# Cached values streamed 256 columns at a time against zero-padded probabilities

## The reference

```
z = rms_norm(x) @ w_in           # q, k, v: 12 heads of 64; GLU value and gate; two branch gates
A = merged attention of 3 groups of 4 heads, (window, dilation) = (128,1), (512,4), (2048,16); @ w_att
B = GLU -> causal depthwise conv (31) -> layer norm -> silu -> @ w_conv_out
x = x + (sigmoid(ga) * A + sigmoid(gb) * B) @ w_out
x = x + SwiGLU(rms_norm(x))
# for the samples, per group g, with cached and new keys and values behind each other:
idx = L + arange(S)[:, None] - dil * arange(window // dil + 1)[None, :]
s = einsum('bshd,bsjhd->bshj', q, k[:, idx]) * HEAD_DIM ** -0.5
o = einsum('bshj,bsjhd->bshd', exp(s - lse), v[:, idx])
o_att = sum over groups of softmax(lse over groups) * o
```

## Time and profile before

| | us |
|---|---|
| median of 3 runs | 1867.36 |
| lowest, highest | 1859.78, 1868.85 |
| the profiled execution | 1867.65 |
| its span in the profile | 1865.9 |
| PE busy | 1780.9 |
| DVE, ACT, POOL busy | 1046.3, 458.9, 69.9 |

### The profile page before, as it was taken

The page is one execution under the profiler, slowest core; times in us unless marked ns, Lnnn a source line. Parts: engine busy times, 40 slices in busy tenths (PEclk is TensorE's granted clock), DMA queues, the critical chain, the costliest instruction groups (busy, mean ns, idle before and its releaser), DMA issues.

```text
span 1865.9 us, 25207 instructions
## 1 busy us (share of the span) xinstructions
PE 1780.9 (95%) x10357; PEld 1671.8 (90%) x10357; DVE 1046.3 (56%) x1464; ACT 458.9 (25%) x900; POOL 69.9 (4%) x125
## 2 busy tenths in 40 slices
PE   6999989999999988989998999999999999999999
PEld 5899989999988888979987789899899899899897
DVE  5688988788987766585304432424424424424425
ACT  5111122323433554512102232121121121121120
POOL 0000000000000011110110000000000000000000
PEclk9999999999999999999579999999999999999999
DMA  6111233234242357865524002222222222222232
GB/s 190 53 60 56 94 120 115 91 114 152 94 138 90 134 168 246 286 212 192 188 78 147 1 34 91 91 91 91 91 91 91 91 91 90 91 90 90 92 109 103
DMA packets 156486, 211.54 MB, mean 113 GB/s; under 512 B 9090, under 2 KB 127010, under 8 KB 155603
## 3 DMA queue, kind: packets, MB, share of 16 engines
q1 hardware_dynamic: 145971, 134.01, 23.3%
q0 software_dynamic: 10416, 76.16, 10.9%
HBM read 180.04 MB, written 74.80 MB: 137 GB/s over the span
## 4 chain that ended last, share of the span: by engine, by line
PE 85%; DVE 6%; DMA 3%; DVEq 2%; SPq 1%; issue 1%; ACT 1%; ACTq 0%; POOL 0%; POOLq 0%
PE ps L694 19%; PE ps L695 19%; PE ps L696 19%; PE ps L1137 4%; PE ps L1135 4%; PE ps L1136 4%; PE ps L962 2%; DVE conv L1498 2%; PE ps L1059 2%; PE ps L1061 2%; PE ps L1060 2%; PE ps L908 1%; DMA qb<-scr_q 1%; PE ps L782 1%; SPq L482 1%
## 5 line engine op out<-in xcount | busy, mean ns | idle before, releaser
L694 PE MATMUL ps<-xhi,whi 128*128 128x352 f32 x1200 | 405.8, 338 | 8.6 <-DVEq L1553 7.0
L696 PE MATMUL ps<-xhi,wlo 128*128 128x352 f32 x1200 | 388.2, 323 | 0.0
L695 PE MATMUL ps<-xlo,whi 128*128 128x352 f32 x1200 | 388.1, 323 | 0.0
L694 PE MATMUL ps<-nhi,whi 128*128 128x352 f32 x1056 | 341.3, 323 | 0.0
L695 PE MATMUL ps<-nlo,whi 128*128 128x352 f32 x1056 | 339.0, 321 | 0.0
L696 PE MATMUL ps<-nhi,wlo 128*128 128x352 f32 x1056 | 338.6, 321 | 0.0
L1498 DVE SCALAR_TENSOR_TENSOR conv<-u,vec,conv 128x1024 f32<-128x1024 f32 x240 | 308.4, 1285 | 25.6 <-issue 11.1
L1454 DVE TENSOR_TENSOR wlo<-raw,whi 128x1024 fp32r<-128x1024 f32 x126 | 153.6, 1220 | 249.4 <-ACT whi L1225 241.2
L694 PEld LDWEIGHTS ps<-xhi,whi 128*128 128x128 f32 x1200 | 228.4, 190 | 19.3 <-DVEq L1553 7.6
L695 PEld LDWEIGHTS ps<-xlo,whi 128*128 128x128 f32 x1200 | 228.7, 191 | 4.2
L696 PEld LDWEIGHTS ps<-xhi,wlo 128*128 128x128 f32 x1200 | 228.0, 190 | 0.0
(11 more groups left out here) (214 smaller groups left out, 2085.1 us busy)
## 6 DMA issues: line engine op xcount, KB each, us to landing
kv_sample<-cache_kv_w POOLq DMA_DIRECT2D x32, 1022.0 KB, 6.5
raw<-w_in SPq DMA_DIRECT2D x50, 512.0 KB, 4.6
raw<-w_gate_up SPq DMA_DIRECT2D x44, 512.0 KB, 3.8
scr_z<-zt SPq DMA_DIRECT2D x34, 528.0 KB, 3.2
qb<-scr_q POOLq DMA_DIRECT2D x24, 512.0 KB, 5.6
raw<-w_down SPq DMA_DIRECT2D x22, 512.0 KB, 4.2
kc<-cache_kv_w POOLq DMA_DIRECT2D x16, 512.0 KB, 6.9
vc<-cache_kv_w POOLq DMA_DIRECT2D x16, 512.0 KB, 4.3
```

Of the source, the lines that this page charges most:

```text
L694: pe_mm(out, wh, rhs_hi, start=first, stop=False)
L695: pe_mm(out, wh, rhs_lo, start=False, stop=False)
L696: return pe_mm(out, wl, rhs_hi, start=False, stop=last)
```

## The change

The roles of the two operands are exchanged. The cached values of one query (128 rows by all 256 columns) now stream, and the probabilities are the weights: 32 columns, of which only the 4 (or 16) of the sequence and query at hand are not zero. The output is 32 partitions by 256 columns, one row for each sample, query and head: two sequences share a block of 32 partitions, and all matmuls of the two add into it. POOL makes the zero-padded weights (`ptz`, `ptz0`) from `ptr`, after the issue of the first three loads, and PE waits for that (`s_pz`). Each row holds the values of all four heads, of which one is wanted: DVE picks it with four multiply-adds with a per-partition mask (`rowhead`), onto the part of the new values (`sample_rows`), and PE turns the rows by one transpose behind the next output unit (`sample_turn`). The tiles are spread as 10 single ones, three pairs and twice four, and end behind output unit 1 instead of 2. Two more tiles of x wait for `s_pv`, since `ptz` lies in their place, and the norm weights wait for the turn.

```diff
+    ptz = at("ptz", [P, 2, NS, 32], F32, S3 + (KT - 5) * D * 4)
+    ptz0 = at("ptz0", [P, DEC_B, 32], F32, S3 + KT * D * 4)
+    orow = at("orow", [P, 2, HD], F32, o_band + 3 * P * 4)
+    rowhead = rs9[:, 12:16]
...
-    VTILES = [0] * 3 + [1] * 13 + [4, 4, 3]
+    VTILES = [0] * 3 + [1] * 10 + [2] * 3 + [4, 4]
...
-        for t in range(KT - 3):
+        for t in range(KT - 5):
             residual_load(t)
         att_gate_load(2)
         sp.wait_ge(s_pv, 1)
+        for t in range(KT - 5, KT):
+            residual_load(t)
+        sp.wait_ge(s_oT2, 1)
         sp.dma_start(nfw[:, :], ...
-        for t in range(KT - 3, KT):
-            residual_load(t)
         ffn_load(FFN0 + 1)
...
+        def spread_probs():
+            nc.gpsimd.memset(ptz[:, :, :, :], 0.0)
+            nc.gpsimd.memset(ptz0[:, :, :], 0.0)
+            pool.wait_ge(s_ptr, 1)
+            pool.drain()
+            for par in range(2):
+                for g in range(1, NG):
+                    to, of = ptz[:, g - 1, DEC_S * par, 16 * par:16 * par + 4], ptr[:, g, 0, 16 * par:16 * par + 4]
+                    nc.gpsimd.tensor_copy(bass.AP(to.tensor, to.offset, [to.ap[0], [2 * DEC_S * 32, 4], [32 + NH, DEC_S], [1, NH]]),
+                                          bass.AP(of.tensor, of.offset, [of.ap[0], [32, 4], [NH, DEC_S], [1, NH]]))
+                last = nc.gpsimd.tensor_copy(ptz0[:, par:DEC_B:2, 16 * par:16 * par + 16],
+                                             ptr[:, 0, 0, :].rearrange("p (x r) -> p x r", r=16)[:, par:DEC_B:2, :])
+            last.then_inc(s_pz, 1)
...
             cache_tile(vc[n % 3], s_kc[n % 3], 1, n % NG, n // NG)
+            if n == 2:
+                spread_probs()
...
             if n == 0:
-                pe.wait_ge(s_ptr, 1)
+                pe.wait_ge(s_pz, 1)
                 pe.wait_ge(s_oTl, 5)
             pe.wait_ge(s_kc[n % 3], 16 * ((NB + n) // 3 + 1))
+            dst = ps[32 * (b // 2):32 * (b // 2) + 32, 7, 0:GW]
             for s in range(DEC_S if g else 1):
-                w = NH if g else NH * DEC_S
-                col = b * NH * DEC_S + s * NH
-                for hp in range(2):
-                    mm = nc.tensor.matmul(ps[:, 7, hp * P + col:hp * P + col + w], vc[n % 3][:, s if g else DEC_S - 1, hp * P:(hp + 1) * P],
-                                          ptr[:, g, 0, col:col + w], start=n == 0 and hp == 0 and s == 0, stop=False, skip_group_check=True)
+                w = ptz[:, g - 1, DEC_S * b + s, :] if g else ptz0[:, b, :]
+                mm = nc.tensor.matmul(dst, w, vc[n % 3][:, s if g else DEC_S - 1, :], start=b % 2 == 0 and g == 0,
+                                      stop=b % 2 == 1 and g == NG - 1 and s == DEC_S - 1, skip_group_check=True)
...
         def new_values():
             for g in range(NG):
-                for hp in range(2):
-                    mm = nc.tensor.matmul(ps[:, 7, hp * P:(hp + 1) * P], rowv[:, g, :, :].rearrange("p a d -> p (a d)"), ptr[:, g, 1, :],
-                                          start=False, stop=g == NG - 1, skip_group_check=True)
+                mm = nc.tensor.matmul(ps[:, 6, 0:HD], ptr[:, g, 1, :], rowv[:, g, 0, :], start=g == 0, stop=g == NG - 1)
             mm.then_inc(s_pv, 1)
+
+        def sample_turn():
+            pe.wait_ge(s_orow, 1)
+            nc.tensor.transpose(ps[:, 6, P:2 * P], orow[:, :, :].rearrange("p a d -> p (a d)"), ident[:, :]).then_inc(s_oT2, 1)
...
+            if r == V_END + 1:
+                sample_turn()
...
         def sample_hi():
-            act.wait_ge(s_pv, 1)
+            act.wait_ge(s_oT2, 1)
...
-                src = ps[r, 7, (h // 2) * P:(h // 2 + 1) * P].rearrange("p (x h) -> p x h", h=NH)[:, :, h]
+                src = ps[r, 6, P:2 * P].rearrange("p (x h) -> p x h", h=NH)[:, :, h]
...
+        V.tensor_reduce(rowhead, ident[:, :].rearrange("p (x h) -> p h x", h=NH), AX_X, ALU.add)
...
+        def sample_rows():
+            dve.wait_ge(s_pv, 1)
+            V.tensor_copy(orow[:, 0, :], ps[:, 6, 0:HD])
+            for h in range(NH):
+                dve.drain()
+                V.scalar_tensor_tensor(orow[:, 0, :], ps[:, 7, h * HD:(h + 1) * HD], rowhead[:, h:h + 1], orow[:, 0, :], ALU.mult, ALU.add)
+            dve.drain()
+            V.tensor_copy(orow[:, 1, :], orow[:, 0, :]).then_inc(s_orow, 1)
...
                 residual(0, i)
+                if r == V_END:
+                    sample_rows()
```

More of the change, by code:

```diff
@@ L214, in build @@
     vc = [at(f"vc{i}", [P, DEC_S, GW], F32, S3 + (KT - 3 + i) * D * 4) for i in range(3)]
+    ptz = at("ptz", [P, 2, NS, 32], F32, S3 + (KT - 5) * D * 4)
+    ptz0 = at("ptz0", [P, DEC_B, 32], F32, S3 + KT * D * 4)
+    assert (KT * D + DEC_B * 32) * 4 <= REG and 2 * NS * 32 == 2 * D
+    orow = at("orow", [P, 2, HD], F32, o_band + 3 * P * 4)
+    rowhead = rs9[:, 12:16]
     x1s = at("x1s", [NS, D], F32, WO[0] + 2 * KT * 512 * 4)
@@ L261, in build @@
     s_qb = [sem(f"s_qb{i}") for i in range(2)]
-    s_prod, s_sc, s_row, s_rowT, s_rowt, s_snew, s_prow, s_pexp, s_ppT, s_ptr, s_pv, s_kcf, s_osh, s_osl = (
-        sem(n) for n in ("s_prod", "s_sc", "s_row", "s_rowT", "s_rowt", "s_snew", "s_prow", "s_pexp", "s_ppT", "s_ptr", "s_pv", "s_kcf", "s_osh", "s_osl"))
+    s_prod, s_sc, s_row, s_rowT, s_rowt, s_snew, s_prow, s_pexp, s_ppT, s_ptr, s_pv, s_kcf, s_osh, s_osl, s_pz, s_orow, s_oT2 = (
+        sem(n) for n in ("s_prod", "s_sc", "s_row", "s_rowT", "s_rowt", "s_snew", "s_prow", "s_pexp", "s_ppT", "s_ptr", "s_pv", "s_kcf", "s_osh", "s_osl", "s_pz", "s_orow", "s_oT2"))
     s_o12, s_cd, s_cw, s_comb, s_oT, s_oTh, s_oTl = (sem(n) for n in ("s_o12", "s_cd", "s_cw", "s_comb", "s_oT", "s_oTh", "s_oTl"))
@@ L344, in build @@
     N_EARLY = UNITS.index(("out", 5))
-    VTILES = [0] * 3 + [1] * 13 + [4, 4, 3]
+    VTILES = [0] * 3 + [1] * 10 + [2] * 3 + [4, 4]
     V_END = len(VTILES) - 1
-    assert sum(VTILES) == NB and UNITS[V_END] == ("out", 2)
+    assert sum(VTILES) == NB and UNITS[V_END] == ("out", 1)
     w_in = a["w_in"][0]
```

## The result

The changed kernel takes 1856.22 us (median of 20 runs, 1852.46 to 1861.81), the kernel before 1866.51 (20 runs). The ratio is 0.9946, 95% interval 0.9935 to 0.9958: faster by 10.3 us, where 22 were forecast. The profiled execution took 1855.7 us, with a span of 1853.9 (before 1865.9).

The account below looks back on a forecast made before the run. PE bounds the kernel, busy 1780.9 of 1865.9 us. Start 0.6, work 65.6, DMA waits 6.9, clock 4.8 and end 1.65 sum to 79.6 us instead of 102.5, giving 1844.8 us; likeliest range 1838 to 1850.

Parts of the forecast that it names:

- The start: Tile 0 waits for s_pz, taken at 884.5 us; tile 1 starts at 886.0, 0.6 us later than before.
- sign of being wrong: At tile 0's wait for POOL: s_pz coming after 890 us would show the forecast wrong.
- fourth rival: At the start, POOL's spreading is slow beside VectorE's traffic: s_pz at 894, 9 us lost, 1854 us; chance 0.07.
- the likeliest case: From tile 1 to attention unit 16, the summed terms hold: 1845 us, own range 1838 to 1850; chance 0.58.
- Tiles: Cached-value tiles: 0.218 us a record, a long tile 1.74 us against 1.71 now at full clock; no gain at equal clock.
- lower bound of 0.107 us for a record: Cached-value tiles: the low end for a record's price, 1.71/16, what it costs however few its columns.
- Clock: Over the tiles, full level with wide streams except after waits; 1.6 us lost at three places, 4.8 in all.
- third rival: Clock stays at half through the tiles, a long tile 3.48 us; slower than before, 1871 us; chance 0.08.
- the reading by the profile's busy time: Over the tiles, the clock gate follows the profile's PE busy time; then the change buys nothing.
- DMA waits: Tile loads through three buffers: PE waits 1.6 us at units 13 to 15, 4.8 behind the fours, 0.5 for slower landings; 6.9.
- first rival: Tile loads set the pace, 5.3 us each beside gate and x loads, with more clock falls: 1854 us; chance 0.17.
- End: Before attention unit 16: the 1.65 us wait for the sample's low part stays; the turned rows come during tile 3.

Follow-up runs that it names:

- with the semaphore: The changed kernel with a semaphore set by the second memset in place of POOL's drain: 1849.0 us, ratio 0.9898.
- four strips: Semaphore in place of the drain, a long tile's four queries in four 32-partition output blocks, short tiles with 128 weight columns, against the changed kernel: 1834.9 us, 0.9826.

## Why the prediction was wrong, point by point

From the start of tile 1 to attention unit 16 I forecast 79.0 us (79.6 less the start) and the trace has 80.8 (895.18 to 976.01); before it was 102.5. That part of the gain came, 21.6 us. The step that failed is **"The start"**: I forecast tile 1 to be 0.6 us later than before, and it came 9.1 us later (17.9 us behind the first attention unit instead of 8.8). Of the 10.35 us missing in the profiled executions (22.9 forecast, 12.55 in the stage), 8.5 are there and 1.8 in the rest.

*Start, in detail.* I priced the instructions that do work and passed over the drain, which does none: a term put at nothing, and it held POOL for 9.09 us. The diff shows it, and my text has no word on it. `s_pz` came at 892, past the 890 that I had named as a sign of being wrong. The work was priced well: 2304 zeroes and six copies took 3.2 us, 3.9 forecast (3.8 by the rows that I named). My upper bound for it (s_pz at 894) held the time, 892, for another reason than the one I gave, and that the fourth rival's 1854 us lies near the measured 1856 is luck. Its mechanism, POOL slowed by VectorE, is there but small: the memset of 2048 elements took 1.84 us beside two-input instructions of DVE, and the six copies took 2.0 us beside them (882.41 to 884.45 with the semaphore), against 1.1 in the changed kernel, where DVE was idle by then. The estimate of 1.9 us for the zeroes, worked out from the Trainium skill ("GPSIMD Engine Reference", 4.1 Engine selection), is near the two memsets' 2.1 us. Without the drain the kernel takes 1849.0 us, inside the range I gave for the likeliest case and 4 above its value; there the start costs 1.1 us more than before (9.9 against 8.8).

*Tiles.* "At equal clock the tiles gain nothing": right, and a little worse than nothing: 0.23 us a record instead of 0.218, 1.84 us a long tile where the old form took 1.71. The units rose from 1.04 to 1.15, as the first product behind a tile and the first record of a tile start later. Against the forecast that is 1.6 us more for the 16 long tiles and 1.2 for the 11 units. The lower bound of 0.107 us for a record was none for 32 weight columns: with 4 streamed columns such a record took 0.04 us (0.34/8).

*Clock.* Right in direction and size, and shown by the wide streams in the kernel before. The third rival, half level, has fallen; so has the reading by the profile's busy time, since the wide streams had the higher clock at the lower busy time. The losses that I put at 1.6 us for each of three waits were 3.0 us in the 6.3 us at 0.53 behind the long wait (half of it ahead of tile 1) and 1.7 at 917 to 923, so 3.2 from tile 1 on where I had 4.8; behind the two waits of 2.5 and 2.2 us between the output units there was none (1.00 from 938 to 960).

*DMA waits.* 6.9 forecast, 7.4 measured:

```profile
PE ps L984 <- POOL ptz L674: 10.9, 1, 10.9
PE ps L984 <- DMA vc<-cache_kv_w: 7.4, 4, 2.5
```

with 2.54 and 2.15 in the fours, as worked out (2.4 twice), and 2.08 at 917, where the load ran beside the gate of chunk 2. The first rival was wrong here, but gains ground once the tiles are short (14.1 us of waits with four strips).

*End.* Right: 1.65 us stay, and the turn is hidden. DVE's picking took 1.94 us (963.08 to 965.02), 1.5 forecast, and the turn followed 3.5 us later. The spread of the tiles is worth nothing either way.

That widening the streams was enough for the clock I hadn't seen as a rival of the change itself. The kernel before with streams of 128 columns reaches 0.9903: even without its drain the changed kernel is no faster (0.9898), within the intervals. The wide version adds other sequences' sums and would need zeroes in the other columns to be of use, which wasn't tried; but it shows that the clock alone, at equal tile costs, is worth as much as the whole gain of the change without its drain. The change of roles by itself paid only when its four matmuls went to four strips.

## What to carry to other kernels

Price the instructions that only order (here a drain on GpSimd) like those that work, above all where an engine on the path waits behind them; a semaphore between producer and consumer ordered them with a gap of 0.14 us. Where a stretch is busy but at half clock, widen or shorten its narrow products before redesigning them, and test the clock with a version that only streams more. If weights are padded to 32 columns, give neighbouring matmuls different blocks of 32 output partitions.

## What the runs showed of the hardware that I had not expected

A drain on GpSimd behind two memsets held its queue for 5.39 us with nothing in flight on any DMA queue, 5.39 with SP's loads alone, 5.64 with its own three loads alone and 9.09 with both (one execution each); a semaphore cost under 0.2 us of gap. Four f32 matmuls with 32 weight columns and 256 streamed ones took 0.57 us on four strips, 1.84 on one. Runs of 4-column products with 128-column weights, 3.27 us long at half clock, went with a clock of 0.59 over the tiles; with 32-column weights, 0.34 us long, it was 0.83, waits included. At full clock an f32 record with 128 weight columns cost 0.107 us with 4 streamed columns (1.71/16) and 0.106 with 128 (1.70/16).
